# The first pairs of weight blocks of an encoder step: four tiles grown together by pieces, a row norm and a load order moved

## The reference

```python
def rms_norm(x, g):
    y = xf * lax.rsqrt(jnp.mean(xf * xf, axis=-1, keepdims=True) + EPS)
    return y * g

def macaron_half(x, g, w_in, w_out):
    a, b = jnp.split(rms_norm(x, g) @ w_in, 2, axis=-1)
    return x + 0.5 * ((jax.nn.silu(a) * b) @ w_out)
```

## Time and profile before

| what | us |
|---|---|
| median of 3 runs | 1278.88 |
| lowest and highest | 1278.86, 1279.47 |
| profiled execution, its own time | 1280.21 |
| span of its trace | 1278.4 |
| TensorE busy in the span | 1265.4 |
| VectorE, ScalarE, GpSimd busy | 741.6, 561.2, 174.8 |

### The profile page before, as it was taken

How to read it: one execution, slowest core, us unless ns; L and a number is a source line. 1 busy time by engine, 2 the same in 40 slices (tenths; PEclk the granted TensorE clock), 3 DMA queues, 4 the chain that set the end, 5 groups by cost and what they waited for, 6 DMA issues and landing times.

```text
span 1278.4 us, 22446 instructions
## 1 busy us (share of the span) xinstructions
PE 1265.4 (99%) x8784; PEld 1243.9 (97%) x8784; DVE 741.6 (58%) x1128; ACT 561.2 (44%) x827; POOL 174.8 (14%) x208
## 2 busy tenths in 40 slices
PE   9999999999999999999999999999999999999999
PEld 8999999999998999999999999999997899999999
DVE  7756574555677656554454675554446756656433
ACT  7534363353275533333343453433345763343322
POOL 0300020046143100000122000000124510000000
PEclk9999999999999999999999999999999999999999
DMA  8454445553203444444443533454451144343443
GB/s 279 163 160 150 161 139 174 195 188 132 100 34 130 164 151 145 160 163 139 151 164 123 196 133 138 157 164 160 135 187 34 55 144 159 137 164 131 135 140 128
DMA packets 39661, 187.45 MB, mean 147 GB/s; under 512 B 4369, under 2 KB 14353, under 8 KB 24497
## 3 DMA queue, kind: packets, MB, share of 16 engines
q1 hardware_dynamic: 38272, 183.38, 41.8%
q0 software_dynamic: 1184, 3.13, 1.1%
q10 hardware_dynamic: 144, 0.11, 0.0%
HBM read 179.70 MB, written 6.90 MB: 146 GB/s over the span
## 4 chain that ended last, share of the span: by engine, by line
PE 95%; DVE 2%; ACT 1%; issue 1%; DMA 1%; SPq 0%; ACTq 0%; DVEq 0%
PE bank L490 29%; PE bank L492 29%; PE bank L491 29%; PE bank L752 1%; PE bank L713 1%; PE bank L890 1%; PE bank L755 1%; PE bank L722 1%; DVE wlo L1526 1%; DMA raw<-in_w_ffn_in 1%; ACT whi L1120 0%; PE outs L516 0%; ACT ew L1281 0%; PE outs L518 0%; PE outs L500 0%
## 5 line engine op out<-in xcount | busy, mean ns | idle before, releaser
L490 PE MATMUL bank<-xhi,whi 128*128 128x320 f32 (+1 forms) x1760 | 545.8, 310 | 3.0 <-DVE wlo L1901 1.1
L492 PE MATMUL bank<-xhi,wlo 128*128 128x320 f32 (+1 forms) x1760 | 543.0, 309 | 0.0
L491 PE MATMUL bank<-xlo,whi 128*128 128x320 f32 (+1 forms) x1760 | 543.0, 309 | 0.0
L1526 DVE TENSOR_TENSOR wlo<-raw,whi 128x2048 fp32r<-128x2048 f32 (+1 forms) x177 | 364.1, 2057 | 230.2 <-ACT whi L1120 230.1
L1120 ACT ACTIVATE whi<-raw 128x2048 fp32r<-128x2048 f32 (+1 forms) x177 | 304.1, 1718 | 242.3 <-PE bank L492 237.9
L490 PEld LDWEIGHTS bank<-xhi,whi 128*128 128x128 f32 x1760 | 330.5, 188 | 6.2 <-issue 3.4
L491 PEld LDWEIGHTS bank<-xlo,whi 128*128 128x128 f32 x1760 | 330.6, 188 | 0.5
L492 PEld LDWEIGHTS bank<-xhi,wlo 128*128 128x128 f32 x1760 | 330.5, 188 | 0.0
L490 PE MATMUL bank<-hhi,whi 128*128 128x320 f32 x704 | 219.0, 311 | 0.0
L492 PE MATMUL bank<-hhi,wlo 128*128 128x320 f32 x704 | 217.5, 309 | 0.0
L491 PE MATMUL bank<-hlo,whi 128*128 128x320 f32 x704 | 217.5, 309 | 0.0
(11 more groups left out here) (233 smaller groups left out, 1041.5 us busy)
## 6 DMA issues: line engine op xcount, KB each, us to landing
raw<-in_w_ffn_in SPq DMA_DIRECT2D x86, 1024.0 KB, 4.8
raw<-in_w_ffn_out SPq DMA_DIRECT2D x64, 704.0 KB, 4.2
raw<-in_w_in_a SPq DMA_DIRECT2D x10, 1024.0 KB, 4.8
raw<-in_w_out SPq DMA_DIRECT2D x8, 1024.0 KB, 4.9
raw<-in_w_kv SPq DMA_DIRECT2D x6, 1024.0 KB, 4.8
raw<-in_w_mkv SPq DMA_DIRECT2D x4, 1024.0 KB, 4.7
raw<-in_w_in_b SPq DMA_DIRECT2D x4, 1024.0 KB, 4.7
raw<-in_w_ffn_in SPq DMA_DIRECT2D x8, 256.0 KB, 7.2
```

What stands on the lines that cost most here:

```text
L490: mm(acc, wh, mhi(ks[q]), start=start and q == 0, stop=False)
L491: mm(acc, wh, mlo(ks[q]), start=False, stop=False)
L492: last = mm(acc, wl, mhi(ks[q]), start=False, stop=stop and q == nk - 1)
L1526: tt(wlo[slot][:, 0:size], raw[slot][:, 0:size], f32(whi[slot][:, 0:size]), ALU.subtract).then_inc(lo_ready[slot], 1)
```

## The change

- **Pieces.** A list START cuts the 8 k-tiles into five pieces: one, one, two, two, two. For each piece SyncE's queue issues x, slot 0's weights and slot 1's weights. The first piece of slot 1 is issued from ScalarE's queue. ScalarE and VectorE split slot 0 and slot 1 of a piece one after the other. TensorE takes each piece for all four tiles before the next. The 8 squares and 7 sums stand behind the five pieces.
- **Layout.** `xT` and `memT` come as 128 rows, in each of which the k-tiles lie side by side, so that a piece of x is one longer row per partition (one tile 1280 bytes, two tiles 2560) and `memT` is one row of 8 KB.
- **Pair 1.** Its block 0 is loaded in halves: the first when three pieces of slot 0 are split (`d_third`), the second when all are. ScalarE copies the first half when TensorE has done with the same half of pair 0 (`first_half`). Then come the second half and slot 1, on both engines ahead of the row norm; they no longer stand among the gates and ups of pair 0.
- **Row norm.** TensorE's product of `ssum` stands after tile 0 of pair 1, not inside pair 0.
- **Banks.** Tiles 0 and 1 of pair 1 go to banks 4 and 5 and wait for no freed bank. The bias product stands after tile 3 of pair 1 and writes bank `outs`.
- **Waits.** ScalarE's wait ahead of `hhi` is for the early constants (`d_early`). GpSimd issues its tables when block 0 of pair 1 is there. The warm-up has 15 products.

The diff, cut to its core (unchanged helpers, declarations of semaphores and the old forms of rewritten loops are left out where the new ones show them):

```diff
+START = [(0, 1), (1, 2), (2, 4), (4, 6), (6, 8)]
+LAST = len(START) - 1
...
 
 
-            x_v = a["xT"].rearrange("(k p) r -> p k r", p=P)
-            for q in range(4):
-                sp.dma_start(x[:, 2 * q:2 * q + 2], x_v[:, 2 * q:2 * q + 2]).then_inc(d_x[q], 16)
-                sp.dma_start(raw[0][:, 512 * q:512 * (q + 1)], weights["in0"][0][:, 512 * q:512 * (q + 1)]
-                             ).then_inc(d_piece[q] if q < 3 else landed[0], 16)
-            for q in range(4):
-                sp.dma_start(raw[1][:, 512 * q:512 * (q + 1)], weights["in0"][1][:, 512 * q:512 * (q + 1)]
-                             ).then_inc(d_piece1[q] if q < 3 else landed[1], 16)
-            load_stage("in0", 1, 2)
-            sp.dma_start(memt[:], a["memT"].rearrange("(k p) r -> p k r", p=P)).then_inc(d_mem, 16)
...
+            x_v = a["xT"]
+            for q, (k0, k1) in enumerate(START):
+                own = slice(256 * k0, 256 * k1)
+                sp.dma_start(x[:, k0:k1], x_v[:, k0:k1]).then_inc(d_x[q], 16)
+                sp.dma_start(raw[0][:, own], weights["in0"][0][:, own]
+                             ).then_inc(d_piece[q] if q < LAST else landed[0], 16)
...
+                if q:
+                    sp.dma_start(raw[1][:, own], weights["in0"][1][:, own]
+                                 ).then_inc(d_piece1[q] if q < LAST else landed[1], 16)
...
+            sp.wait_ge(piece_lo, 3)
+            sp.dma_start(raw[0][:, 0:BLK // 2], weights["in0"][2][:, 0:BLK // 2]).then_inc(d_third, 16)
+            sp.wait_ge(lo_ready[0], 1)
+            sp.dma_start(raw[0][:, BLK // 2:BLK], weights["in0"][2][:, BLK // 2:BLK]).then_inc(landed[0], 16)
+            sp.wait_ge(lo_ready[1], 1)
+            sp.dma_start(raw[1][:], weights["in0"][3]).then_inc(landed[1], 16)
+            sp.dma_start(memt[:], a["memT"]).then_inc(d_mem, 16)
...
-                    for slot, some, all_ in ((0, piece_lo, lo_ready[0]), (1, piece1_lo, lo_ready[1])):
-                        for q in range(4):
-                            if slot == 1 and q == 2:
-                                row_norm(stage, R)
-                            pe.wait_ge(all_, 1) if q == 3 else pe.wait_ge(some, q + 1)
-                            if slot == 0:
-                                pe.wait_ge(xn_lo, 2 * q + 2)
+                    for q, (k0, k1) in enumerate(START):
+                        pe.wait_ge(xn_lo, k1)
+                        for slot, some in ((0, piece_lo), (1, piece1_lo)):
+                            if q == LAST:
+                                pe.wait_ge(lo_ready[slot], 1)
+                            else:
+                                pe.wait_ge(some, q + 1)
...
+                                               part=range(k0, k1))
+                                if q == LAST:
                                     last.then_inc(acc_ready, 1)
+                            if slot == 0 and k1 == KD // 2:
+                                last.then_inc(first_half, 1)
...
+                        spare = halves and j < 2
+                        if not spare:
+                            wait_acc(t0 + 4 * i + j)
...
+                        product(banks[4 + j if spare else j][:, 0:R], slot, col, 256, range(KD), KD,
...
-                    body(1, False, lambda j: stats() if j == 1 else None, halves=True)
+                    body(1, False, lambda j: row_norm(stage, R) if j == 0 else stats() if j == 3 else None, halves=True)
...
-            for _ in range(19):
+            for _ in range(15):
                 mm(aux[1][:, 0:R], mixhi[:, 0, 0:P], mixhi[:, 0, :], start=True, stop=True)
...
-                mm(banks[4][0:H_A, 0:NREL + 1], table[:], hot[:], start=True, stop=True).then_inc(trel_ready, 1)
+                mm(HS[0:H_A, 0:NREL + 1], table[:], hot[:], start=True, stop=True).then_inc(trel_ready, 1)
...
-                act.wait_ge(d_const, CONST)
+                act.wait_ge(d_early, 16)
...
-                        if c == 1:
+                        if c == 1 and not (stage == "in0" and isinstance(i, int) and i == 0):
...
+            act.dma_start(raw[1][:, 0:256], weights["in0"][1][:, 0:256]).then_inc(d_piece1[0], 16)
...
+            for q, (k0, k1) in enumerate(START):
+                own = slice(256 * k0, 256 * k1)
...
+                for k in range(k0, k1):
...
+                act.wait_ge(d_piece[q] if q < LAST else landed[0], 16)
+                nc.scalar.activation(whi[0][:, own], raw[0][:, own], ACT.Copy
+                                     ).then_inc(piece_hi if q < LAST else hi_ready[0], 1)
+                act.wait_ge(d_piece1[q] if q < LAST else landed[1], 16)
+                nc.scalar.activation(whi[1][:, own], raw[1][:, own], ACT.Copy
+                                     ).then_inc(piece1_hi if q < LAST else hi_ready[1], 1)
+            for k in range(KD):
+                nc.scalar.activation(sq8[:, k, :], x[:, k, :], ACT.Square).then_inc(sq_ready, 1)
...
+            act.wait_ge(d_third, 16)
+            act.wait_ge(first_half, 1)
+            nc.scalar.activation(whi[0][:, 0:BLK // 2], raw[0][:, 0:BLK // 2], ACT.Copy).then_inc(third_hi, 1)
             act.wait_ge(landed[0], 16 * (PAIR0["in0"] + 1) + 16)
             act.wait_ge(acc_ready, TILE0["in0"] + 2)
...
+            nc.scalar.activation(whi[0][:, BLK // 2:BLK], raw[0][:, BLK // 2:BLK], ACT.Copy).then_inc(hi_ready[0], 1)
+            split_hi(1, PAIR0["in0"] + 1, BLK, acc_ready, TILE0["in0"] + 4)
             row_norm("in0", R)
-            nc.scalar.activation(whi[0][:, BLK // 2:BLK], raw[0][:, BLK // 2:BLK], ACT.Copy).then_inc(hi_ready[0], 1)
...
+                    spare = stage == "in0" and isinstance(i, int) and i == 1
...
+                        tt(gate[:, c, :], banks[4 + c if spare else c][:, 0:R], r[:], ALU.mult).then_inc(acc_free, 1)
...
-                        if c == 1:
+                        if c == 1 and not (stage == "in0" and isinstance(i, int) and i == 0):
...
+            for q, (k0, k1) in enumerate(START):
+                own = slice(256 * k0, 256 * k1)
+                inputs_lo("in0", "ffn1_0", lambda k: x[:, k, :], R, tiles=range(k0, k1))
...
+                tt(wlo[0][:, own], raw[0][:, own], f32(whi[0][:, own]), ALU.subtract
+                   ).then_inc(piece_lo if q < LAST else lo_ready[0], 1)
+                if q < LAST:
...
+                tt(wlo[1][:, own], raw[1][:, own], f32(whi[1][:, own]), ALU.subtract
+                   ).then_inc(piece1_lo if q < LAST else lo_ready[1], 1)
+            for k in range(1, KD):
...
             dve.wait_ge(third_hi, 1)
             tt(wlo[0][:, 0:BLK // 2], raw[0][:, 0:BLK // 2], f32(whi[0][:, 0:BLK // 2]), ALU.subtract
                ).then_inc(third_lo, 1)
+            dve.wait_ge(hi_ready[0], PAIR0["in0"] + 2)
+            tt(wlo[0][:, BLK // 2:BLK], raw[0][:, BLK // 2:BLK], f32(whi[0][:, BLK // 2:BLK]), ALU.subtract
+               ).then_inc(lo_ready[0], 1)
+            split_lo(1, PAIR0["in0"] + 1, BLK)
             row_norm("in0", R)
...
+                    ts(trel[:], HS[0:H_A, 0:NREL + 1], 1.0 / SCALE, None, ALU.mult).then_inc(bias_in, 1)
...
-            pool.wait_ge(landed[1], 16)
+            pool.wait_ge(landed[0], 32)
...
-    o["xT"] = np.concatenate([a["x_prompt"][0].T, a["x_sample"][0].T], axis=1)
-    o["memT"] = a["mem_prompt"][0].T
+
+    xT = np.concatenate([a["x_prompt"][0].T, a["x_sample"][0].T], axis=1)
+    o["xT"] = xT.reshape(KD, P, R).transpose(1, 0, 2)
+    o["memT"] = a["mem_prompt"][0].T.reshape(KD, P, N_MEM).transpose(1, 0, 2)
```

More of the change, by code:

```diff
@@ L349, in encoder_kernel @@
         d_mem = sem("d_mem")
-        d_piece = [sem(f"d_piece{q}") for q in range(3)]
-        d_piece1 = [sem(f"d_piece1{q}") for q in range(3)]
+        d_piece = [sem(f"d_piece{q}") for q in range(LAST)]
+        d_piece1 = [sem(f"d_piece1{q}") for q in range(LAST)]
         piece1_hi = sem("piece1_hi")
         ones_there = sem("ones_there")
+        d_third = sem("d_third")
+        first_half = sem("first_half")
         third_hi = sem("third_hi")
@@ L364, in encoder_kernel @@
         d_early = sem("d_early")
-        d_x = [sem(f"d_x{q}") for q in range(4)]
+        d_x = [sem(f"d_x{q}") for q in range(LAST + 1)]
         d_const = sem("d_const")
@@ L618, in each @@
                                 pe.wait_ge(xn_lo, x0 + k + 1)
-                        product(banks[j][:, 0:R], slot, col, 256, range(KD), KD,
+                        product(banks[4 + j if spare else j][:, 0:R], slot, col, 256, range(KD), KD,
                                 lambda k: xhi[:, k, :], lambda k: xlo[:, k, :], True, True, each
@@ L1403, in _ @@
                     input_hi(x[:, k, :], xhi[:, k, :], "ffn1_0", k)
-                act.wait_ge(d_piece[q] if q < 3 else landed[0], 16)
-                nc.scalar.activation(whi[0][:, 512 * q:512 * (q + 1)], raw[0][:, 512 * q:512 * (q + 1)], ACT.Copy
-                                     ).then_inc(piece_hi if q < 3 else hi_ready[0], 1)
-            def squares(tiles):
```

(36 more changed lines are left out.)

26 lines of the change are left out of this document (5 added, 21 removed).

## The result

The changed kernel takes 1284.88 us (median of 6 runs, 1283.78 to 1285.97); the kernel before, 1279.05 in the same comparison (6 runs, 1278.86 to 1279.47). The ratio is 1.0045, with a 95% interval of 1.0033 to 1.0057: **slower by 5.8 us**, more than the 0.2% that this kernel's measurement can tell. The profiled execution of the changed kernel took 1284.84 us, its span is 1282.9, against 1280.21 and 1278.4.

The account below looks back on a forecast made before the run. TensorE, 95% of the chain, was taken as the bound, with block pair 2's start deciding: 20.8 for block pair 1 plus 19.8 gives 40.6, 1.7 us later than 38.91, so 1280.6 against the median 1278.88; range 1279.1 to 1283.0.

Parts of the forecast that it names:

- the clock behind the new gap: TensorE's idle before block pair 2, forecast at 3.9 us; the forecast case added nothing for a lower clock behind it.
- carrying the shift to the median: Final sum: 1.7 us later, set against the median 1278.88, which is 1.33 below the profiled execution, giving 1280.6.
- a later row sum: TensorE, behind the first tile of block pair 1: the row sum was to end 4.06 us after that pair's start.
- the own time: Profiled execution's own time, 1280.21 against a span of 1278.4; the same 1.7 us was added to both.
- Start of the stream: Kernel start: first real product at about 5.6, 1.6 us sooner; block pair 1 at 20.8, between 19.6 and 21.8.
- The chain behind the row sum: From the row sum's end through ScalarE's and VectorE's steps to block pair 2's start: 15.75 us.
- Rival 1: Clock falls in TensorE's new gap before block pair 2, costing 2.6 us more: 1283.2; chance 0.17.
- Rival 2: Kernel start: pieces land no sooner, first product stays at 7.2, block pair 1 at 22.8: 1282.6; chance 0.14.
- Rival 3: Block pair 2 doesn't hang on the row sum's chain, starts at 36.7, 2.2 us won: 1276.7; chance 0.07.
- What the prediction called free: Spare banks, later GpSimd tables, moved bias product, ScalarE's early-constants wait, shorter warm-up and memT's layout: claimed to cost nothing.

Follow-up runs that it names:

- e1_filled: The changed kernel with 22 unused products added on TensorE behind the bias product, filling the gap before block pair 2: 1283.65 us, ratio 1.0035.

## Why the prediction was wrong

It said 1280.6 (1279.1 to 1283.0), no difference as the likeliest, and it is 1284.88. The step that failed is the clock behind the new gap, which the sum had at nothing and which cost 2.1 of the 4.3 us missed. Some 1.1 more come from carrying the shift to the median, 0.4 from a later row sum and 0.1 to 0.2 from the own time.

- **Start of the stream: right.** First real product 5.64, taken 5.6. Block pair 1 at 21.1, taken 20.8.
- **The chain behind the row sum: right, step by step.** 15.82 us against 15.75: r, `up`, both `hid`, memlo, gates and the last low split stand within 0.1 us of their forecast places behind it. Tile 2 waits 0.57 (taken 0.45), the idle is 3.73 (3.9). Block pair 2 starts at 41.12, forecast 40.6: 2.2 later than in the profile of before, forecast 1.7. Of the 0.5, 0.4 is the row sum's end, 25.30 where 24.86 was forecast.
- **The clock: the step that failed, 2.1 us.** Rival 1 was worked out, with its place and its price (2.6 us, measured 2.1), and got 0.17. What spoke against it was the products at the warm step right behind 1.13 us of idling. But that says nothing of a gap three times as long. No row bore on 3.9 us. The page of the Trainium skill named there ("TensorE: Matmul & The Clock Gate", section "Why this matters for your kernels") did speak to it, with its warning against idle gaps between bursts. The trace of after (0.50 behind 3.73 us) and e1_filled (1.00 with the gap filled) agree with the warning. A rival with a sound price that only lacks a row at the size in question deserves more than 0.17: as the likeliest case it would have given 1283.2, still 1.7 short.
- **Carrying the sum to the median: a second failure, 1.1 us.** The shift was worked out against the profiled execution of before, and then 1.33 was taken off. But the 1.13 us of idling at 10.31 in the earlier trace rows, which I counted as won by the change, was longer than usual in that execution: there ScalarE had waited 1.28 us for its piece. In four other profiles of the old front the first product starts at 6.72 to 6.85 (7.20), and the third group at 8.99 to 9.54 (10.31), in three of them behind 0.49 to 0.65 us of idling. In the usual execution the old front is 0.9 us faster, and the row sum at 18.3. A gain that lies in an unusual wait of the profiled run can't be added to a median that doesn't contain the wait. The profiled time, 1.33 above the median, had said that something in it was late.
- **The rest**: own time less span is 2.0 us in after, 1.8 in before. That is 0.1 to 0.2 which the sum had at nothing.
- Rival 2 (pieces late) didn't come. Rival 3 (faster) didn't; the rows that left no slack in the chain were read rightly. What the prediction called free (spare banks, GpSimd's later tables, the bias product, ScalarE's wait) shows no cost: span less start is 2.3 us larger in after, and 2.1 of that are the clock.

With what was measured afterwards the sum comes out at: usual delay 3.2, clock 2.1, own time 0.2, on 1279.1, that is 1284.6. The 0.3 left isn't explained.

## What to carry over

If a change makes a new idle of TensorE, ask not only how long it is but whether it is longer than any that the trace shows with the clock still up. If it is longer, put the price of the slow restart into the likeliest case. Before a gain at a kernel's start is credited, compare the profiled run's time with the median: if it is an unusually long one, find the wait that makes it so, and don't count that wait as won. And a step that is moved out of one chain takes its neighbours along: the row sum behind a tile cost 3.5 us (24 products) and gave back 2.5, because slot 1's split left the chain with it.
